# The state chain of a pair of heads moved into the product bursts of the next pair, with two sets of chain operands, v centred where it is transposed, and channel sums as rounded halves

## The reference, cut to what matters

```
def rwkv7_scan(r, decay, k, v, a_vec, b_vec):          # per head, state is 64 x 64
    def step(state, inp):
        r_t, w_t, k_t, v_t, a_t, b_t = inp
        sa = einsum('bhij,bhj->bhi', state, a_t)
        state = state * w_t[..] + sa[..., None] * b_t[..] + v_t[..., None] * k_t[..]
        return state, einsum('bhij,bhj->bhi', state, r_t)

kk = kk * rsqrt(max(sum(kk * kk), 1e-24))               # key sums, per head
o = rwkv7_scan(rh, dh, kh, vh, -kk, kk * ah)
mean = mean(o); var = mean(square(o - mean))            # per head
o = (o - mean) * rsqrt(var + GN_EPS) * ln_w + ln_b
bonus = sum(rh * kh * r_k) * vh                         # key sums
return o + bonus
aq = rms_norm(aq, a_q_g); ak = rms_norm(ak, a_k_g)      # query sums, 128 channels
ya = chunked_band_attention(aq, ak, av, bias) * silu(az)
```

## Time and profile before

| | us |
|---|---|
| median of 3 runs | 2415.3 (2412.42 to 2416.1) |
| the profiled execution | 2410.3 |
| its span | 2408.6 |
| PE busy | 2350.2 (98%) |
| DVE busy | 1508.9 (63%) |
| ACT busy | 1102.8 (46%) |
| mean granted clock of PE | 0.993 |

### The profile page before, as it was taken

The page is one execution under the profiler, slowest core; times in us unless marked ns, Lnnn a source line. Parts: engine busy times, 40 slices in busy tenths (PEclk is TensorE's granted clock), DMA queues, the critical chain, the costliest instruction groups (busy, mean ns, idle before and its releaser), DMA issues.

```text
span 2408.6 us, 54358 instructions
## 1 busy us (share of the span) xinstructions
PE 2350.2 (98%) x21920; PEld 2293.3 (95%) x21920; DVE 1508.9 (63%) x2072; ACT 1102.8 (46%) x1455; POOL 12.8 (1%) x27
## 2 busy tenths in 40 slices
PE   6999999999999999997999999999999999999999
PEld 6898999999999999996899999999989999999999
DVE  7556776666546766666866666676576555555554
ACT  5343445555434555434444444444465444444442
POOL 0000000000000000000000000000000000000000
PEclk9999999999999999998999999999999999999999
DMA  6453555555555555554343333333445365555654
GB/s 232 145 185 111 175 184 188 186 187 188 189 187 189 187 188 186 182 183 149 129 134 120 127 119 134 127 127 124 169 147 175 117 203 189 188 189 187 190 189 160
DMA packets 110235, 401.34 MB, mean 167 GB/s; under 512 B 12378, under 2 KB 12405, under 8 KB 109952
## 3 DMA queue, kind: packets, MB, share of 16 engines
q1 hardware_dynamic: 108000, 390.91, 48.9%
q0 software_dynamic: 2080, 8.06, 1.0%
HBM read 396.81 MB, written 2.10 MB: 166 GB/s over the span
## 4 chain that ended last, share of the span: by engine, by line
PE 95%; DVE 3%; ACT 1%; issue 0%; DMA 0%; SPq 0%; DVEq 0%; ACTq 0%
PE bank L428 94%; DVE scratch L1440 1%; DVE w_lo L1391 1%; ACT w_hi L967 0%; DVE h_lo L1437 0%; DMA x<-in_xT 0%; DVE cum L1437 0%; PE bank L742 0%; DVE ping L1437 0%; DVE root L1479 0%; DVE acc L1437 0%; PE bank L691 0%; DVE sq L1437 0%; DVE x L1437 0%; DVE croot L2034 0%
## 5 line engine op out<-in xcount | busy, mean ns | idle before, releaser
L1391 DVE TENSOR_TENSOR w_lo<-raw,w_hi 128x1024 fp32r<-128x1024 f32 x736 | 896.4, 1224 | 707.9 <-ACT w_hi L967 703.4
L967 ACT ACTIVATE w_hi<-raw 128x1024 fp32r<-128x1024 f32 x736 | 779.0, 1060 | 959.8 <-PE bank L428 947.5
L428 PE MATMUL bank<-h_hi,w_hi 128*128 128x256 f32 x4016 | 1148.6, 286 | 20.0 <-DVE h_lo L1437 8.5
L428 PE MATMUL bank<-h_lo,w_hi 128*128 128x256 f32 x4016 | 1125.0, 280 | 0.0
L428 PE MATMUL bank<-h_hi,w_lo 128*128 128x256 f32 x4016 | 1123.4, 280 | 0.0
L428 PEld LDWEIGHTS bank<-h_hi,w_hi 128*128 128x128 f32 x4016 | 758.4, 189 | 35.0 <-issue 12.7
L428 PEld LDWEIGHTS bank<-h_lo,w_hi 128*128 128x128 f32 x4016 | 758.8, 189 | 3.2 <-issue 2.2
L428 PEld LDWEIGHTS bank<-h_hi,w_lo 128*128 128x128 f32 x4016 | 758.3, 189 | 0.0
L428 PE MATMUL bank<-m_hi,w_hi 128*128 128x256 f32 x704 | 196.5, 279 | 0.0
L428 PE MATMUL bank<-m_lo,w_hi 128*128 128x256 f32 x704 | 196.5, 279 | 0.0
L428 PE MATMUL bank<-m_hi,w_lo 128*128 128x256 f32 x704 | 196.5, 279 | 0.0
(11 more groups left out here) (404 smaller groups left out, 2714.1 us busy)
## 6 DMA issues: line engine op xcount, KB each, us to landing
raw<-in_units SPq DMA_DIRECT2D x736, 512.0 KB, 3.3
x<-in_xT SPq DMA_DIRECT2D x4, 512.0 KB, 5.9
memx<-in_memT POOLq DMA_DIRECT2D x4, 512.0 KB, 7.5
out_y<-obuf SPq DMA_DIRECT2D x8, 256.0 KB, 4.5
bias_t<-in_bias POOLq DMA_DIRECT2D x8, 192.0 KB, 3.1
dft<-in_dft POOLq DMA_DIRECT2D x1, 1024.0 KB, 8.4
decay<-in_decay POOLq DMA_DIRECT2D x1, 768.0 KB, 6.5
inv<-in_inv POOLq DMA_DIRECT2D x1, 512.0 KB, 3.9
```

The costliest lines, as they stand in the source:

```text
L428: return pe.matmul(out, lhsT, rhs, start=start, stop=stop, skip_group_check=True)
L967: return act.activation(out, in_, ACT.Copy, scale=scale)
L1391: dve.tensor_tensor(w_lo[slot][:, :, :], raw[slot][:, :, :], w_hi[slot][:, :, :].bitcast(F32), ALU.subtract).then_inc(split_done, 1)
```

## The change

What it does, by engine:
- PE: the chain of pair g-1 runs in the bursts of pair g. After unit 0: `state(0)`, `output(0)`; after 1: `solve(1)`; 2: `state(1)`, `output(1)`; 3: `solve(2)`; 4: `state(2)`, `output(2)`; 5: `solve(3)`; 6: `output(3)`. The first pair has no chain in its bursts; the last pair has that of the pair before in its bursts, and its own between half units 8 to 11 (`last_chain`).
- Two sets of chain operands (`chains[0]`, `chains[1]`), used in turn; the loop over pairs is unrolled by two.
- v is multiplied by `center` in place of the identity where it is transposed, so that the output has no mean; the matmul with `center` goes. ACT squares the output from PSUM into two tiles, one of them rounded (`g_hi`), DVE makes the rest (`g_lo`), PE sums both with a rounded ones matrix.
- The key sums (after unit 10 in place of 9) and the query sums (after 13 in place of 12) are made the same way, `two_halves`: high and low part as two matmuls of 512 columns, one accumulation.
- b x (a, r) and k x (a, r), 128 columns, are split: b x a, k x a after unit 0, b x r, k x r after unit 4.
- The step of `normed_output` on DVE, of the pair before, stands ahead of `units(10)`.

```diff
+        CHAIN = ("Vt", "Bt", "Kk", "SA0", "sol", "BKb", "BKk", "r", "bon", "bz")
+        chains = [{n: place(...) for n, kb in zip(CHAIN, places[j])} for j in range(2)]
-        STATE = (4, 2)
-        OUT = (3, 5)
+        STATE = (2, 6)
+        OUT = (6, 2)
     # PE
+            def two_halves(ones):
+                mm(banks[7][:, :], ones[:, :], s_hi[...], True, False)
+                return mm(banks[7][:, :], ones[:, :], s_lo[...], False, True)
-                if k == 9 and half != 0:
-                    pe.wait_ge(keys_ready, n.next("keys"))
-                    mm(banks[7][:, 0:T], con_("head_ones"), small["sq"][:, :])
-                    mm(banks[7][:, T:2 * T], con_("head_ones"), small["rk"][:, :]).then_inc(head_sums, 1)
-                if k == 12:
+                if k == 10:
+                    pe.wait_ge(keys_split, n.next("keys"))
+                    two_halves(head_r).then_inc(head_sums, 1)
+                if k == 13:
                     pe.wait_ge(sums_read, n.next("sums"))
-                    pe.wait_ge(qk_squared, n.next("qk"))
-                    mm(banks[7][:, :], con_("ones"), qr[...]).then_inc(qk_sums, 1)
+                    pe.wait_ge(qk_split, n.next("qk"))
+                    two_halves(ones_r).then_inc(qk_sums, 1)
     # PE, late: the first two bursts
                 units(0)
                 from_dve()
+                if chain:
+                    state(0)
+                    output(0)
-                p, q = corners(product(b4(3), m["b"], both), product(b4(5), m["k"], both))
+                p, q = corners(product(b64(3), m["b"], a_), product(b64(5), m["k"], a_))
-                p, q = corners(product(b64(4), a_, m["b"]), product(b64(2), v_, eye))
+                p, q = corners(product(b64(4), a_, m["b"]), product(upper64(7), v_, less_mean))
...
                 units(1)
+                if chain:
+                    from_dve()
+                    solve(1)
...
-                p, q, r = corners(product(b64(5), m["Kt"], m["Vt"]), product(b64(6), a_, eye), product(b64(2), m["b"], eye))
+                p, q = corners(product(b64(5), m["Kt"], of(w["Vt"])), product(b64(7), m["b"], eye))
...
+                units(6)
+                if chain:
+                    from_dve()
+                    output(3).then_inc(psum_for_act, 1)
...
+                if g < HEADS_A - 1:
+                    units(8)
+                    if chain:
+                        squares_sum()
+                    from_act(2)
+                    for k in range(9, 16):
+                        units(k)
+                else:
+                    squares_sum()
+                    last_chain(units)
+            def squares_sum():
+                from_dve()
+                mm(banks[5][:, 0:T], head_r[:, :], g_hi[:, :], True, False)
+                mm(banks[5][:, 0:T], head_r[:, :], g_lo[:, :], False, True).then_inc(psum_for_act, 1)
     # ACT, start: the rounded ones matrices
+            copy(ones_r[:, :], con_("ones"))
+            copy(head_r[:, :], con_("head_ones")).then_inc(ones_rounded, 1)
     # ACT, heads
                 if k == 7:
                     act.wait_ge(keys_ready, n.next("keys"))
+                    to_dve(copy(s_hi[:, :, :], sqrk[:, :, :]))
                     copy(small["pv"][:, 1:257], p2(1)[:, 0, :])
...
-                if k == 9:
+                if k == 10:
                     from_dve()
                     to_dve(act.activation(small["sq"], small["sq"], ACT.Sqrt))
                 if k == 11:
                     act.activation(qr[:, :, :], p2(0), ACT.Square)
+                    act.activation(s_hi[:, :, :], p2(0), ACT.Square).then_inc(qk_squared, 1)
     # ACT, late: between units(5) and units(6)
                 units(5)
+                if chain:
+                    squared_outputs()
+                keep(w["Kk"], banks[4])
+                units(6)
+            def squared_outputs():
                 psum()
+                for h in range(2):
+                    act.activation(small["gsq"][HALVES[h], :], out_of(h), ACT.Square)
+                for h in range(2):
+                    act.activation(g_hi[HALVES[h], :], out_of(h), ACT.Square)
+                copy(small["o"][HALVES[0], :], out_of(0))
+                to_dve(copy(small["o"][HALVES[1], :], out_of(1)))
     # DVE, heads
                 if k == 8:
                     from_act()
+                    low(s_lo[:, :, :], sqrk[:, :, :], s_hi[:, :, :]).then_inc(keys_split, 1)
+                    from_act()
...
-                if k == 9:
+                if k == 10:
                     dve.wait_ge(head_sums, n.next("sums"))
                     to_act(ts(sm["sq"], banks[7][:, 0:T], 1e-24, None, ALU.max))
                     settle()
                     tt(sm["rk"], banks[7][:, T:2 * T], sm["v"][:, :], ALU.mult).then_inc(sums_read, 1)
-                if k == 10:
+                if k == 11:
                     from_act()
                     step(dve.reciprocal(sm["sq"], sm["sq"]))
                     settle()
                     step(tt(sm["kk"][:, :], sm["kk"][:, :], sm["sq"], ALU.mult))
+                    dve.wait_ge(qk_squared, n.next("qk"))
+                    low(s_lo[:, :, :], qr[:, :, :], s_hi[:, :, :]).then_inc(qk_split, 1)
                     settle()
                     step(tt(sm["t0"][:, :], sm["kk"][:, :], icl_g, ALU.mult))
     # DVE, late: its end
+                units(6)
+                if chain:
+                    output_low()          # g_lo
                 if prepare:
                     prepare()             # keys_of
+                units(7)
+                if prepare:
+                    units(8)
+                    units(9)
+                    if chain:
+                        normed_output(g - 1, 1 - par)
+                    for k in range(10, 16):
+                        units(k)
+                    return
```

More of the change, by code:

```diff
@@ L675, in late, with heads @@
-            def late(units):
+            def two_halves(ones):
+                mm(banks[7][:, :], ones[:, :], s_hi[:, :, :].rearrange("p s t -> p (s t)"), True, False)
+                return mm(banks[7][:, :], ones[:, :], s_lo[:, :, :].rearrange("p s t -> p (s t)"), False, True)
+            def heads(k):
+                part(k)
+                if k == 10:
+                    pe.wait_ge(keys_split, n.next("keys"))
+                    two_halves(head_r).then_inc(head_sums, 1)
+                if k == 13:
+                    pe.wait_ge(sums_read, n.next("sums"))
+                    pe.wait_ge(qk_split, n.next("qk"))
+                    two_halves(ones_r).then_inc(qk_sums, 1)
@@ L677, in late @@
+            def late(units, g):
+                w = chains[g % 2]
+                chain = g > 0
+                state, output, solve = chain_of(chains[1 - g % 2])
+                m = {name: of(t) for name, t in bd.items()}
+                a_ = lambda hs, c: small["a"][hs, c * CHUNK:(c + 1) * CHUNK]
+                v_ = lambda hs, c: small["v"][hs, c * CHUNK:(c + 1) * CHUNK]
                 units(0)
                 from_dve()
-                m = {name: of(t) for name, t in bd.items()}
-                a_ = lambda hs, c: a_rt[hs, c, 0, :]
@@ L751, in late @@
[L751 to L757, removed]
+                from_act()
+                p, q = corners(product(b64(3), m["b3"], m["F"]), product(b64(4), m["k"], eye))
+                p.then_inc(psum_for_dve, 1)
+                q.then_inc(psum_for_act, 1)
@@ L843, in _ @@
                     from_act(2)
-            for _ in range(HEADS_A - 1):
-                late(heads)
-            late(part)
+            for g in range(HEADS_A - 1):
+                late(heads, g)
+            late(part, HEADS_A - 1)
             def channel_sums(src, bank=7):
@@ new lines, in late @@
+                keep(w["Kk"], banks[4])
+                units(6)
+                keep(w["sol"], banks[3])
+                keep(w["SA0"], banks[4])
+                units(7)
+                if tail:
+                    output_root()
+                    for k in range(8, 11):
+                        units(k)
+                    from_dve()
+                    squared_outputs()
+                    for k in range(11, 14):
+                        units(k)
+                    output_root()
+                    for k in range(14, 16):
+                        units(k)
+                else:
+                    units(8)
+                    if chain:
+                        output_root()
+                    for k in range(9, 16):
+                        units(k)
@@ L1293, in _ @@
                     to_dve(copy(spare[:, 1:2], icl[:, 0, 0:1]))
-            with n.loop(HEADS_A - 1, {"psum": 21, "dve": 3} | pair_counts) as i:
-                late(lambda k: heads(k, i + 1))
-            late(queries)
+            late(lambda k: heads(k, 1, 1), 0, chain=False)
+            with n.loop((HEADS_A - 2) // 2, {"psum": 38, "dve": 4} | pair_counts) as i:
```

(20 more changed lines are left out.)

449 lines of the change are left out of this document (242 added, 207 removed).

## The result

The changed kernel takes 2423.0 us (median of 20 runs, 2414.9 to 2429.8) where the kernel before takes 2415.2 in the same session (20 runs, 2410.1 to 2423.7): ratio 1.0034, 95% interval 1.0025 to 1.0044. It is slower by 0.34%. Measured again (experiment 10) the ratio is 1.0020 (1.0000 to 1.0039), so the loss is small and its size is known to a few us only. The forecast was 2424. The profiled execution has a span of 2417.0 us against 2408.6, 8.4 more.

A forecast was written before the change was run, and what follows sets the result against it. TensorE (PE) was taken to bound the kernel, 95% of the span. Terms -26.2 + 21.0 + 13 + 3.4 = +11.2 gave 2421.5 us, or 2426.5 by the median; predicted 2424, forecast's own range 2414 to 2432, with rivals 2392 to 2436.

The forecast's parts named there:

- Work on PE: On PE over the pairs: moved chain, dropped `center` product and rounded sums save 26.2 us, 3.67 on each full pair.
- the sums: Key and query sums on PE: four rounded 512-column passes replace two plain ones, 0.79 us less a pair, -5.5 in all.
- the seven visits: PE leaving the unit stream for the chain's small matrices: seven times 0.34 us saved per pair, 2.4, in all -16.7.
- The path: From `output(3)` through ACT and DVE to `qk_split`: 26.9 us against PE's 23.3; 3.5 of wait in six pairs, +21.0.
- The clock: Behind the six waits at the query sums PE's clock drops to half, costing 13 us.
- 2.2 x 6: Clock loss of 2.2 us behind each of six query-sum waits, taken from two earlier waits that lost 2.8 and 1.7.
- Before the loop: Heads of pair 0 wait on DVE behind the prefix sums: +3.4 us, from 0 to 6, including 2.2 of clock.
- The last step of the prediction: Choosing 2424 us, between 2421.5 from the profiled execution and 2426.5 from the median of the runs shown.
- A: At the query sums, the wait comes but the clock stays up, or drops only now and then: 2408.5 to 2413.5, chance 0.21.
- B: DVE's queue is not late at `qk_split`, so PE's saved work is the time: 2387.5 to 2392.5, chance 0.17.
- C: The path to the query sums is longer: wait 4.2 and more, clock 2.8 each, 2429 to 2434, chance 0.09.
- D: Bursts wait inside for ACT or DVE, so the visits are not saved: up to 17 us more, 2438, chance 0.03.

The follow-up runs named there:

- experiment 10: The changed kernel itself measured once more, nothing altered, to see behind which waits the clock falls: 2421.0 us, ratio 1.002 to the kernel before.
- Experiment 7: The changed kernel with `normed_output` moved behind units(12) and `s_lo` taken ahead of the reciprocal: 2387.6 us, ratio 0.9887 to the kernel before.
- experiment 9: The kernel before with only v centred where it is transposed, the product with `center` removed: 2411.2 us, ratio 0.9979 to the kernel before.
- experiment 4: The changed kernel with nine needless matmuls on PE ahead of the query-squares wait in six pairs: 2412.3 us, ratio 0.9988 to the kernel before.
- experiments 1: The changed kernel with `normed_output` moved behind units(12) instead of ahead of units(10): 2396.4 us, ratio 0.9924 to the kernel before.
- experiment 2: The changed kernel with `normed_output` one unit later, between units(10) and units(11): 2411.2 us, ratio 0.9985 to the kernel before.

## Why the prediction was right, by its own steps

**Work on PE, forecast -26.2.** Experiment 7 shows it bare. Its six full periods are 3.72 shorter than before (68.86 to 65.14), forecast 3.67. Its first pair saves 5.9 (63.08 for 68.97), the six 22.3, and the last costs 2.4 (69.26 for 66.85): -25.8. By part: the product with `center` 0.43 a pair (experiment 9), as priced; the sums 0.85 where 0.79 stood. A rounded pass of 512 columns takes 0.23 to 0.25 (query sums in experiment 7: 1380.69 and 1380.94, next unit 1381.18), so the 0.23 of the sum was the right price and not the 0.216 beside it. What is left of a period is 3.72 - 0.43 - 0.85 = 2.44 for the seven visits, the squares' sum and the split products together, forecast 2.40 + 0.20 - 0.13 = 2.47. These three were not taken apart.

**The path, forecast 26.9 against 23.3.** From the first matmul of `output(3)` (1294.29) to the query sums (1321.21) it is 26.92. The steps measured 4.3, 5.5, 2.2, 9.4, 1.4 and 4.1 where 3.8, 5.6, 2.2, 9.6, 1.5 and 4.2 stood. PE's own side was 0.45 too short: the burst from `output(3)` to the next unit takes 2.12 (to 1296.41), where 1.73 had been put together; the twelve instructions of `output(3)` itself (12 x 0.0293 = 0.35) had been left out. Hence a wait of 3.15 for the 3.5 taken, 18.9 us for 21.0.

**The clock, forecast +13.** The mechanism was right, and experiment 4 isolates it: 8 to 11 us between the ratios, 8.6 in the profiled execution (1.6, 2.6, 0, 0, 1.6 and 2.8 over an undisturbed 68.29). The mis-sized step is "2.2 x 6". The two waits that it was taken from had both been followed by half clock, and of twelve such waits, seen in two executions, only nine were; those nine lost 1.8 us each.

**Before the loop, forecast +3.4.** The path was right: PE goes on with the query sums 34.5 us after the wait for `icl` (1190.29 - 1155.80), as forecast (1188.0 - 1153.46). But the 2.2 of clock in this term did not come in the profiled execution, where no half clock followed the wait of 2.42 us; from the wait for `icl` to the first transposes it lost 0.5 (45.54 for 45.06). In experiment 10 it followed a wait of 3.53 us there, and the stretch lost 2.0.

**Not in the sum:** the waits for `m_No`, 2.2 us.

By the trace, from the wait for `icl` to the next stage: -25.8 + 18.9 + 8.6 + 0.5 + 2.2 = +4.4, and 4.5 were read, against the forecast +11.2. So the forecast had every main mechanism, and its sum was 7 us too high for this stretch: 4.4 at the clock, 2.9 before the loop, 2.1 at the wait, less the 2.2 that it had left out and 0.4 on PE.

That 2424 came out 1 us from the median is therefore in good part luck. The profiled execution lost another 4.0 us outside this stretch, and about 3.4 of them are half clock that came at places which the change does not touch. The last step of the prediction, to take 2424 between 2421.5 and 2426.5, took off another 2.5 without a reason in the kernel. What the medians show over the +4.4 (8.2 us with 6.0 to 10.6, and 4.8 with 0 to 9.4 in experiment 10) is not taken apart. All ten traces of kernels with the chain moved have the half clock behind that wait for ACT (1910.85 in the changed kernel), and the two with the chain in its old place have not. Whether that is chance stays open.

**The rivals.** A and B were built. A (the wait without the clock) is experiment 4: 2412.3, in its 2408.5 to 2413.5. B (DVE in time) is what experiments 1 and 7 make of the change: 2396.4 lies above its 2387.5 to 2392.5 and 2387.6 at the lower edge; it needed 3.15 us off the path. C (a wait of 4.2 and more) and D (waits inside the bursts) did not come; of D there is the 0.9 at `m_No`, in two pairs. The dividing line of A was put wrongly: "nearer 2.2 and drops it now and then" was to cost nothing, and experiment 2, at 1.97, lost 1.6 us in five of six pairs.

## What to carry to other kernels

When a piece of work is moved, follow the longest way from it through the other engines' queues up to the next instruction of the busy engine that needs it, with everything that stands ahead in each queue, and compare that with the busy engine's own time between the two points; here 26.9 against 23.8 turned 26 us of saved work into 5 to 8 lost. Then look on that way for what nobody waits for (`normed_output`, the reciprocal) and put it behind: no work was changed, and 32 to 35 us came back. In this kernel a recorded wait of TensorE of 2.9 us cost 4.5 us in the mean and one of 1.97 cost 3.6, clock included, 1.6 and 1.8 times its length. Try a repair that only shortens it: from 2.9 to 0.8 it gave 20 to 23 us where the waits were 13.

## What was not expected of the hardware

- Half clock came behind waits of PE as short as 1.97 us, in five of six; behind 0.76 to 0.80 us in none of twelve; behind 2.9 us in nine of twelve. The wait of 1.6 us for `icl` was not followed by it in any of twelve traces. Equal waits in one execution were followed by 0, 3.4 or about 6 us at 0.50.
- Even outside the pairs, in code that is the same in all kernels, a wait of 1.74 us with one of 0.69 right behind it was followed by half clock in ten traces and not in two.
- Nine needless matmuls in the idle time kept the clock at 1.00 behind all six waits and made the kernel faster, by 8 to 11 us.
- DVE stood for 2.2 to 5.2 us at the jump back of its loop, with nothing to wait for, at both jumps of seven traces (32 packets on the instruction queue) and not in two with the same loop (22).
